# Latent prompt attention: the order of the sixteen softmax units of a head pair, long, long, short, short against long, short, long, short

## The reference, cut to what matters

```python
def q_block(args):                       # 128 queries, block n of 8
    qn_i, qr_i, n = args
    sc = (einsum('bqhd,bshd->bhqs', qn_i, kn) + einsum('bqhr,bsr->bhqs', qr_i, kr)) * scale
    qpos = n * 128 + arange(128)
    sc = where(kpos[None, :] <= qpos[:, None], sc, NEG_INF)
    p = softmax(sc, axis=-1)
    return einsum('bhqs,bshd->bqhd', p, v)
```

## Time and profile before

| | |
|---|---|
| median of 3 timed runs | 3064.36 us (3059.7 to 3064.64) |
| profiled execution | 3051.96 us |
| its span | 3050.2 us |
| PE busy in the span | 2355.8 us, 77% |
| DVE, ACT busy | 920.0 us, 655.8 us |
| turns (L1995), PE matmuls | 576 of them, 280 ns each |
| row maxima (L1944), DVE | 128, mean 758 ns |
| exponentials (L1873), ACT | 128, mean 744 ns |

### The profile page before, as it was taken

The page is one execution under the profiler, slowest core; times in us unless marked ns, Lnnn a source line. Parts: engine busy times, 40 slices in busy tenths (PEclk is TensorE's granted clock), DMA queues, the critical chain, the costliest instruction groups (busy, mean ns, idle before and its releaser), DMA issues. The chain is left out here.

```text
span 3050.2 us, 28070 instructions
## 1 busy us (share of the span) xinstructions
PE 2355.8 (77%) x9994; PEld 1111.6 (36%) x9994; DVE 920.0 (30%) x2385; ACT 655.8 (22%) x1328; POOL 163.7 (5%) x162
## 2 busy tenths in 40 slices
PE   5888867876878888477878888777789688888870
PEld 2444434443323333144434444343344433333220
DVE  2444432453211111123215555421234422111114
ACT  2444430111111111133224444311111111111101
POOL 0000000000111111000000000000000011111100
PEclk9999976996989999788989999978889699999995
DMA  4000024217999999433120000021062599999956
GB/s 156 14 14 8 4 98 150 72 67 290 419 419 418 416 416 403 184 108 109 49 62 11 21 21 11 24 56 47 16 225 73 219 370 419 418 416 414 415 239 249
DMA packets 149256, 575.11 MB, mean 189 GB/s; under 512 B 37730, under 2 KB 63330, under 8 KB 96754
## 3 DMA queue, kind: packets, MB, share of 16 engines
q1 hardware_dynamic: 99170, 494.58, 41.0%
q10 hardware_dynamic: 30384, 42.92, 4.0%
q0 software_dynamic: 19568, 35.86, 3.1%
HBM read 534.95 MB, written 73.96 MB: 200 GB/s over the span
## 5 line engine op out<-in xcount | busy, mean ns | idle before, releaser
L1446 PE MATMUL m_ps_gu<-ring,m_xT 128*64 128x512 f32 x2080 | 551.5, 679 | 135.2 <-issue 129.6
L1446 PEld LDWEIGHTS m_ps_gu<-ring,m_xT 128*64 128x64 f32 x2080 | 170.4, 154 | 438.2 <-issue 431.2
L1355 PE MATMUL m_ps_y<-w_o,oT_all 128*128 128x512 f32 x512 | 248.9, 644 | 26.7 <-DMA w_o<-mla_w_o 13.2
L1455 PE MATMUL m_ps_y<-ring,m_hT 128*64 128x512 f32 x1040 | 237.5, 598 | 27.1 <-DVE m_hT L1319 26.6
L1312 DVE TENSOR_TENSOR m_h<-m_act,m_ps_gu 128x256 f32<-128x256 f32 x64 | 38.6, 604 | 648.1 <-ACT m_act L1064 648.1
L546 PE MATMUL a_ps_q<-a_w,a_hT 128*128 128x512 f32 x384 | 193.4, 648 | 2.0 <-ACT a_hT L326 0.7
L1064 ACT ACTIVATE m_act<-m_ps_gu 128x256 f32<-128x256 f32 x64 | 24.6, 384 | 664.2 <-PE m_ps_gu L1446 664.2
L1355 PEld LDWEIGHTS m_ps_y<-w_o,oT_all 128*128 128x128 f32 x512 | 104.3, 209 | 150.3 <-issue 137.0
L1988 PE MATMUL h_ps_s<-h_kT,h_qT 96*128 96x512 f32 (+3 forms) x384 | 147.2, 492 | 1.4 <-DVE h_kT L1911 1.4
L1995 PE MATMUL h_ps_p<-ident,h_p 128*128 128x128 f32 x576 | 88.2, 280 | 57.3 <-ACT h_pT L1882 28.4
L1873 ACT ACTIVATE h_p<-h_ps_s,h_nm 128x128 f32<-128x128 f32 (+7 forms) x128 | 95.2, 744 | 149.2 <-DVE h_nm L1945 145.0
(11 more groups left out here) (370 smaller groups left out, 2776.3 us busy)
## 6 DMA issues: line engine op xcount, KB each, us to landing
ring<-moe_w_gate SPq DMA_DIRECT2D x130, 1024.0 KB, 21.1
ring<-moe_w_up SPq DMA_DIRECT2D x130, 1024.0 KB, 24.7
ring<-moe_w_down SPq DMA_DIRECT2D x130, 1024.0 KB, 19.2
x_ffn<-misc ACTq DMA_DIRECT2D x18, 512.0 KB, 4.9
normed<-m_y ACTq DMA_DIRECT2D x18, 512.0 KB, 2.6
p_yr<-expert_rows SPq DMA_DIRECT2D x9, 1024.0 KB, 5.7
f_yr<-expert_rows SPq DMA_DIRECT2D x9, 1024.0 KB
g_cp<-cache_mla_latent SPq DMA_DIRECT2D x64, 128.0 KB, 2.0
```

The lines of the kernel that those rows point to most:

```text
L1355: ins = eng.matmul(ps_y[:, n, :], oT_all[:, k, P * t:P * t + P], w_o[:, k, 512 * n:512 * n + 512], start=k == 0, stop=k == KC - 1)
L1446: ins = eng.matmul(gu_now[r], xT_now[:, i, r], w[:, slot, s, 0:2, DE * i:DE * i + DE], start=i == 0, stop=i == KC - 1)
L1455: ins = eng.matmul(ps_y[r, n, :], hT[:, i, r], w[:, slot, s, 2, D * i + 512 * n:D * i + 512 * n + 512], start=i == 0, stop=i == 1)
```

## The change

The order of the units within each group of eight. A pair of blocks (7 and 0, 6 and 1, 5 and 2, 4 and 3) is now gone through once for head 0 and once for head 1, where before each block was done for both heads in a row.

```diff
     GROUPS = ((7, 0, 6, 1), (5, 2, 4, 3))
     PLACE = {6: 0, 7: 1, 0: 2, 1: 3, 2: 0, 3: 1, 4: 2, 5: 3}
-    UNITS = [(g, n, s) for g in range(2) for n in GROUPS[g] for s in range(2)]
+    UNITS = [(g, n, s) for g in range(2) for i in range(0, 4, 2) for s in range(2) for n in GROUPS[g][i:i + 2]]
     NU = len(UNITS)
```

## The result

The changed kernel takes 3093.68 us (median of 4 runs, 3090.31 to 3097.61) against 3064.03 before: ratio 1.0100, 95% interval 1.0083 to 1.0118. It is slower, as forecast, but by twice the 14 us of the prediction, and outside its range.

The account below looks back on a forecast made before the run. No engine was taken as full, TensorE nearest, with waits between engines. Six inner pairs 8.5 + first pair 4.0 + last 1.5 = + 14 us on 3064.4 gave 3078.5 us, range 3066 to 3086.

Parts of the forecast that it names:

- Link prices: Times per step of a unit (scores to mask, mask to exponentials, exponentials to turn, turn), by key blocks, independent of the order.
- the long chain: Scores, statistics and exponentials of a long unit all lie between two long turns: 5.39, 4.94 or 5.63 us.
- an inner pair: One of six pairs between the first and last: from 47.43 to 48.85 us, + 1.42 each, 8.5 in all.
- The term from turn(4) to turn(8): Second stretch of an inner pair, TensorE waiting for long units: 10.33 us against 9.13 before, + 1.20.
- The gain at the head: Start of a pair: turn(1) no longer waits for a delayed copy out; turn(0) to turn(4) 12.20 us against 12.50.
- the first pair: First pair of the phase, no values parts or reciprocals in its first half to cover waits: + 4.0 us.
- the last one: Last pair of the phase, without keys, ending on a turn that waits for a copy out: taken as + 1.5 us.
- The stall ahead of the first turn: TensorE idle about 2.4 us before each pair's first turn, released by the exponentials.
- The clock falls in the longer stalls: Rival: TensorE's clock drops to 0.88 in the phase, 37 us more in eight pairs, 3115 us; chance 0.04.
- Nothing follows from it: Phase stands between barriers, its one transfer a pair ahead: the added 14 us is neither hidden nor has consequences.
- The covered chain: Rival: TensorE's other work covers the waits between long turns; pair 43.7 us, about 3034 us; chance 0.06.
- no change: Rival: hand-offs between engines come out 0.1 us shorter; pair 47.6 us, 3067 us; chance 0.11.

Follow-up runs that it names:

- h_mid: Kernel before with only the second four units of each pair alternating (8, 8, 1, 1, 7, 2, 7, 2, rest as before); 3071.57 us, ratio 1.0047.
- a_fill: Changed kernel plus unread products on TensorE in the stalls ahead of each pair's first turn, ahead of turn(8) and in the first pair; 3063.83 us, ratio 1.0022.
- a_first: Changed kernel with scores(m + 2) made ahead of turn(m), not behind it, at u = 4, 6 and 14; 3065.68 us, ratio 1.0014.
- a_fill_head: Changed kernel plus unread products at heads of pairs and in the first pair's first half only, stall ahead of turn(8) left open; 3071.42 us, ratio 1.0049.
- a_again: Changed kernel, unchanged, measured again on another chip beside the kernel before; 3099.65 us, ratio 1.0133.
- h_head: Kernel before with only the first four units of each pair alternating (8, 1, 8, 1, rest as before); 3083.36 us, ratio 1.0086.
- b_stall: Kernel before plus two copies on ScalarE ahead of the exponentials of each pair's first unit, from the second pair on; 3066.62 us, ratio 1.0025.

## Why the prediction was wrong

- **Link prices and the long chain: right.** With the clock held an inner pair is 48.62 us (48.85 forecast). The term from turn(4) to turn(8), + 1.20, is what `h_mid` measures by itself. The gain at the head is there too: turn(0) to turn(4) is 12.08 instead of 12.50.
- **That the phase came out 13.7 us longer, for 14, is in part luck.** By `a_fill` the first pair is 3.7 us longer (4.0 forecast), the six inner ones 7.1 (8.5), the last one 3.0 (1.5), and 1.7 of these 3.0 are a fall near the end. Without it the order costs 12.
- **The stall ahead of the first turn: right in length** (2.4 forecast, 2.50 measured), **wrong in what it does.** The step that failed is the clock, put at nothing in the sum and given a chance of 0.04 as the rival "The clock falls in the longer stalls". It makes the other 30 us of the phase (423.3 against 393.5 of `a_fill`). The rival was priced at 37, the right size. Its chance was put down for two reasons, and neither holds. That the full clock holds with stalls of up to 1.4 us says nothing of 2.4. And "the one fall beside this phase" is not the only one: the 0.88 from which the rival took its price is four falls behind stalls of 1.4 and 2.1 us, in the same profile. So the trace did bear the rival out, for stalls shorter than 2.4 us, where the prediction said that it neither did nor excluded it.
- **"Nothing follows from it" failed for the same reason.** The chain's added time is TensorE's idle time, and it was counted as worth its own length only. In the changed kernel 13.7 us of it in the phase brought 29.8 more.
- **The base.** The prediction took the clock of 1.00 in one profile for the phase's property. In a second profile of the same kernel it fell in the first pair.
- **Rivals.** The covered chain (pairs of 43.7 us) and no change (47.6) are both excluded by the 48.62 us of `a_fill`. The result lies 8 us above the range.

The Trainium skill, "TensorE: Matmul & The Clock Gate", section "A second HAM failure mode: psum-queue depth-cycling", describes a kernel in which short idle times between groups of matmuls, often enough, make the clock swing between its two levels. These traces agree: the lower level followed on three stalls of 0.8 to 1.0 us in a row at 3 of 7 heads (`a_first`), on one of 1.8 in 3 of 7 pairs (`a_fill_head`), and on one of 2.5 at 7 of 7 heads (the changed kernel).

## What to carry to other kernels

When buffers alternate by unit number, an order that alternates long and short units puts all long ones on one buffer, and their whole chain between two of them; pair them so that each buffer gets long and short in turn. Price idle time that a change adds to TensorE twice: its length, and a fall of the clock behind it, also where one profile of the phase shows none. Before that, look at the rest of the same trace for the shortest stall that a fall stands behind. Where stalls can't be removed, products that nobody reads, written to a free bank, are a cheap test of the clock's share, and here, in the kernel before, even a small gain (0.14%).

## What was not expected of the hardware

- The clock fell behind stalls much shorter than the 12 us that the prediction named: at 7 of 7 heads behind 2.50 us in the changed order, and again at 7 of 7 in `a_again`; at 5 of 7 behind the same 2.50 in `h_head`; at 3 of 7 behind 2.63 us in the old order (`b_stall`); at 3 of 7 behind 0.96 us with two of 0.78 ahead (`a_first`); in 3 of 7 pairs behind 1.82 (`a_fill_head`). It fell in none of seven pairs with three stalls of 1.2 us (`h_mid`), and at none of 14 heads with 1.0 us in the two profiles of the kernel before. The length of the last stall alone doesn't order these cases.
- A fall costs 1.5 to 1.7 us: pairs of 48.62 and 50.26, 47.61 and 49.12, 46.77 and 48.45 us. One twice as long, as in the pair of `h_head` above, costs 3.2 (51.44 and 48.22).
- Some 2.8 us of unread products in a pair (43.35 busy us in `a_fill` against some 40.5 of `h_mid`, whose pair is as long) cost nothing where the engine was idle.
